# Loading x and context ahead of the constants, and placing the k and q products inside the next chunk's w_ada tiles, in a two-layer float32 kernel

## The reference

```python
sh1, sc1, g1, sh2, sc2, g2 = adaln(c, w_ada, b_ada)          # silu(c) @ w_ada + b_ada, split in 6
h = modulate(rms_norm(x, norm_mix_g), sh1, sc1)               # y * (1 + scale) + shift
csh1, csc1, ... = adaln(c_ctx, w_ada, b_ada)
hc = modulate(rms_norm(ctx, norm_mix_g), csh1, csc1)
q, k, v = split(h @ w_qkv, 3);  qc, kc, vc = split(hc @ w_qkv, 3)
```

## Time and profile before

| | us |
|---|---|
| median of 3 runs (2806.07 to 2807.3) | 2806.37 |
| the profiled execution | 2807.16 |
| its span, first to last instruction | 2805.4 |
| PE busy | 2711.4 (97%) |
| DVE busy | 1580.2 (56%) |
| ACT busy | 1174.5 (42%) |

### The profile page before, as it was taken

One profiled execution on the slowest core, in us unless ns is written; L12 is line 12 of the kernel. 1 busy time (PEld: TensorE's weight loads), 2 busy tenths in 40 slices (PEclk: granted clock), 3 DMA queues, 4 the chain that ended last, 5 costly groups with the idle time before them and its releaser, 6 DMA issues.

```text
span 2805.4 us, 47582 instructions
## 1 busy us (share of the span) xinstructions
PE 2711.4 (97%) x20374; PEld 2564.8 (91%) x20374; DVE 1580.2 (56%) x2407; ACT 1174.5 (42%) x1473; POOL 83.1 (3%) x85
## 2 busy tenths in 40 slices
PE   6999999999979999999999799999999999999999
PEld 3688888889979999999999698999988889999999
DVE  2466766665468765456554665655544555444554
ACT  2233333333345444344543344454535445434443
POOL 0010000000000000000000000000000000000000
PEclk9999999999999999999999799999999999999999
DMA  9955666663548875555555255445444345555554
GB/s 298 356 180 175 205 198 205 204 208 126 168 158 266 257 226 185 181 184 185 181 175 175 93 173 158 151 154 155 142 122 129 120 136 165 181 184 184 172 181 158
DMA packets 382138, 508.79 MB, mean 181 GB/s; under 512 B 40697, under 2 KB 252281, under 8 KB 381927
## 3 DMA queue, kind: packets, MB, share of 16 engines
q1 hardware_dynamic: 380215, 502.17, 55.8%
q0 software_dynamic: 1712, 3.58, 0.6%
HBM read 503.44 MB, written 2.22 MB: 180 GB/s over the span
## 4 chain that ended last, share of the span: by engine, by line
PE 90%; DVE 3%; ACT 3%; issue 2%; DMA 1%; SPq 1%; DVEq 0%; ACTq 0%
PE PG L852 23%; PE PG L853 23%; PE PG L854 23%; PE PG L843 3%; PE PG L845 3%; PE PG L844 3%; ACT wh L1095 1%; PE PS L945 1%; PE PS L861 1%; PE PS L929 1%; SPq L706 1%; PE PX L768 1%; PE PS L872 1%; DMA raw<-in_w_qkv 1%; PE PS L897 1%
## 5 line engine op out<-in xcount | busy, mean ns | idle before, releaser
L1410 DVE TENSOR_TENSOR wl<-raw,wh 128x1024 fp32r<-128x1024 f32 x748 | 917.5, 1227 | 984.4 <-ACT wh L1095 982.2
L1095 ACT ACTIVATE wh<-raw 128x1024 fp32r<-128x1024 f32 x748 | 790.4, 1057 | 1237.6 <-PE PG L854 1017.1
L852 PE MATMUL PG<-HHL,wh 128*128 128x256 f32 (+1 forms) x1696 | 499.7, 295 | 5.9 <-DVE HHL L1537 5.9
L853 PE MATMUL PG<-HHL,wh 128*128 128x256 f32 (+1 forms) x1696 | 488.4, 288 | 0.0
L854 PE MATMUL PG<-HHL,wl 128*128 128x256 f32 (+1 forms) x1696 | 488.3, 288 | 0.0
L852 PE MATMUL PG<-FHL,wh 128*128 128x256 f32 x1376 | 391.7, 285 | 9.0 <-DVE wl L1410 6.9
L853 PE MATMUL PG<-FHL,wh 128*128 128x256 f32 x1376 | 390.9, 284 | 0.0
L854 PE MATMUL PG<-FHL,wl 128*128 128x256 f32 x1376 | 390.8, 284 | 0.0
L852 PEld LDWEIGHTS PG<-HHL,wh 128*128 128x128 f32 (+1 forms) x1696 | 332.9, 196 | 12.2 <-issue 5.8
L853 PEld LDWEIGHTS PG<-HHL,wh 128*128 128x128 f32 (+1 forms) x1696 | 333.0, 196 | 2.5 <-issue 1.9
L854 PEld LDWEIGHTS PG<-HHL,wl 128*128 128x128 f32 (+1 forms) x1696 | 332.7, 196 | 0.1
(11 more groups left out here) (324 smaller groups left out, 5071.4 us busy)
## 6 DMA issues: line engine op xcount, KB each, us to landing
raw<-in_w_in SPq DMA_DIRECT2D x208, 512.0 KB, 3.4
raw<-in_w_up SPq DMA_DIRECT2D x344, 256.0 KB, 3.1
raw<-in_w_ada SPq DMA_DIRECT2D x128, 512.0 KB, 4.6
raw<-in_w_down SPq DMA_DIRECT2D x84, 512.0 KB, 3.6
raw<-in_w_qkv SPq DMA_DIRECT2D x80, 512.0 KB, 4.7
first<-in_w_ada SPq DMA_DIRECT2D x82, 256.0 KB, 7.1
raw<-in_w_o SPq DMA_DIRECT2D x32, 512.0 KB, 3.6
raw<-in_w_in SPq DMA_DIRECT2D x64, 256.0 KB, 3.0
```

Source lines behind the costliest of these rows:

```text
L852: pe.matmul(dst, hi[:, c0:c1], xh, start=step.first and j % per == 0, stop=False, skip_group_check=True)
L853: pe.matmul(dst, hi[:, c0:c1], xl, start=False, stop=False, skip_group_check=True)
L1095: ac.activation(wh[n % NSPL][:, 0:src.shape[1]], src, ACT.Copy).then_inc(S["hi"], 1)
L1410: dv.tensor_tensor(wl[n % NSPL][:, 0:x], src, wh[n % NSPL][:, 0:x], ALU.subtract).then_inc(S["lo"], 1)
```

## The change

x and context are issued first by SP. The condition vectors and the 20 remaining constants are issued by ACT, ahead of its first instruction; the ones matrix is no longer loaded but written by GpSimd. The wait for all the constants moves from the `energy` matmuls to L881. The steps of `early` and the order of the tiles move:

```diff
--- before.py
+++ after.py
@@ -161,9 +161,8 @@
         qkv, rest = mats[KC:n_qkv], mats[n_qkv:]
         plan = []
         for c in range(NCH):
-            plan += chunk_tiles(c)
-            if c:
-                plan += mats[2 * c - 2:2 * c]
+            tiles = chunk_tiles(c)
+            plan += tiles[:2] + (mats[2 * c - 2:2 * c] if c else []) + tiles[2:]
         plan += mats[KC - 2:KC]
         self.start = len(plan)
         late = [t for c in range(2 * D, 5 * D, ADA_W) for t in ada_tiles(c)]
@@ -196,8 +195,8 @@
             for n in range(8 * c, 8 * c + 8):
                 self.at["chunk", n, 0] = len(self.steps)
                 self.steps.append(Step("chunk", n))
-            if c:
-                self.early(c - 1)
+                if c and n % 8 == 3:
+                    self.early(c - 1)
         self.early(NCH - 1)
         for p, (name, g, k0, nk, tiles) in enumerate(self.prods):
             k = 0
@@ -268,8 +267,7 @@
                 P.put(at, 0, "mod", (z, ch), 0)
             for z in "xc":
                 P.put(at, 0, "mod", (z, ch), 1)
-        at = ("chunk", 8 * c + 10, 0) if c < NCH - 1 else ("early", NCH - 2, 0)
-        P.put(at, 0, "split", 2 * c + 1, 0)
+        P.put(("chunk", 8 * c + 8, 0) if c < NCH - 1 else at, 0, "split", 2 * c + 1, 0)
     at = ("early", NCH - 1, 0)
     P.put(at, 0, "split", KC, 0)
     for job, g in (("k_out", 0), ("k_out", 1), ("q_out", 0), ("q_out", 1)):
@@ -674,7 +672,7 @@
     def up_view(g, blk):
         return result("up", g)[:, blk // 2, T * (blk % 2):T * (blk % 2) + T]
 
-    consts = ((ident, "ident"), (ones, "ones"), (means, "means"), (sel, "sel"), (na_mask, "na_mask"), (caus_q, "caus_q"),
+    consts = ((ident, "ident"), (means, "means"), (sel, "sel"), (na_mask, "na_mask"), (caus_q, "caus_q"),
               (caus_k, "caus_k"), (rot, "rot"), (freq, "freq"), (bada, "b_ada"), (gmix, "g_mix"), (gffn, "g_ffn"),
               (gqk, "g_qk"), (g2, "g_in"), (mg, "g_ml"), (glat, "g_lat"), (gn, "g_nope"), (gr, "g_rope"),
               (cw2, "conv2"), (gb, "gate_b"), (rpbt, "rpb"))
@@ -682,13 +680,9 @@
 
     def sync(sp):
         w = Waits(sp)
-        sp.dma_start(CS[:, :, :], I["conds"]).then_inc(S["cond"], 16)
+        sp.dma_start(X[:, :, :], I["xT"].rearrange("(c p) t -> p c t", p=128)).then_inc(S["xload"], 16)
+        sp.dma_start(XC[:, :, :], I["ctxT"].rearrange("(c p) t -> p c t", p=128)).then_inc(S["cload"], 16)
         for i, (kind, name, k, nk, segs) in enumerate(plan):
-            if i == 0:
-                for dst, src in consts:
-                    sp.dma_start(dst[tuple(slice(None) for _ in dst.shape)], I[src]).then_inc(S["const"], 16)
-                sp.dma_start(X[:, :, :], I["xT"].rearrange("(c p) t -> p c t", p=128)).then_inc(S["xload"], 16)
-                sp.dma_start(XC[:, :, :], I["ctxT"].rearrange("(c p) t -> p c t", p=128)).then_inc(S["cload"], 16)
             j = P.slot_before[i]
             if j is not None:
                 n = P.index[j]
@@ -715,12 +709,13 @@
 
     def gpsimd(po):
         w = Waits(po)
+        po.memset(ones[:, :], 1.0).then_inc(S["pool"], 1)
         po.memset(CSP[:, :, :], 0.0).then_inc(S["pool"], 1)
         po.memset(padt[:, :, :], 0.0).then_inc(S["pool"], 1)
-        w.wait_ge(S["pool"], 2)
+        w.wait_ge(S["pool"], 3)
         w.wait_ge(*const_done)
         po.tensor_copy(padt[:, :, 48:79], rpbt[:, :, :]).then_inc(S["pool"], 1)
-        w.wait_ge(S["pool"], 3)
+        w.wait_ge(S["pool"], 4)
         po.dma_start(pad_dram[0:30720].rearrange("(a p n) -> p a n", a=2, n=128), padt[:, :, :]).then_inc(S["pad"], 16)
         w.wait_ge(S["pad"], 16)
         w.wait_ge(*product_done("early", 0))
@@ -865,7 +860,7 @@
             ps = bank(u)
             if (job, phase) == ("energy", 1):
                 z, j = key
-                w.wait_ge(*const_done)
+                w.wait_ge(S["pool"], 1)
                 w.wait_ge(S["energy_sq"], nth("energy", key, 0))
                 for ch in range(4):
                     o = T * (z == "c")
@@ -873,6 +868,7 @@
                                     start=z == "x" and j == 0 and ch == 0, stop=j == 3 and ch == 3, skip_group_check=True)
                 end.then_inc(S["energy"], 1)
             elif (job, phase) == ("rows", 1):
+                w.wait_ge(*const_done)
                 w.wait_ge(S["ada_row"], key + 1)
                 w.wait_ge(S["rx"], 1)
                 if key:
@@ -1362,9 +1358,12 @@
                 ac.activation(VHL[:, 0, 2 * key:2 * key + 2, :], GA[:, 2 * key:2 * key + 2, :],
                               ACT.Copy).then_inc(S["y_hi"], 1)
 
+        ac.dma_start(CS[:, :, :], I["conds"]).then_inc(S["cond"], 16)
+        for dst, src in consts:
+            ac.dma_start(dst[tuple(slice(None) for _ in dst.shape)], I[src]).then_inc(S["const"], 16)
         w.wait_ge(S["cond"], 16)
         ac.activation(CSs[:, :, :], CS[:, :, :], ACT.Silu).then_inc(S["silu_c"], 1)
-        w.wait_ge(S["pool"], 1)
+        w.wait_ge(S["pool"], 2)
         ac.activation(CSP[:, :, 0:2], CS[:, :, :].rearrange("p z k -> p k z"), ACT.Silu).then_inc(S["silu_c"], 1)
         for s, step in enumerate(steps):
             if step.kind == "mat" and step.opens:
@@ -1920,7 +1919,7 @@
 
 def constants():
 
-    c = {"ident": np.eye(128), "ones": np.ones((128, 128))}
+    c = {"ident": np.eye(128)}
     c["means"] = np.tile(1.0 / np.array([2048, 512, 256, 192, 128, 192, 192]), (128, 1))
     c["sel"] = np.stack([np.arange(128) % 32 == z for z in range(2)], 1)
     c["means"][64:, 5] = 0.0
```

## The result

| | before | after |
|---|---|---|
| median of 4 runs each, side by side | 2806.39 us (2806.07 to 2807.3) | 2850.76 us (2843.01 to 2857.13) |
| profiled execution, its span | 2807.16, 2805.4 | 2843.01, 2841.2 |
| L881, now L877, of chunk 0 | 45.23 | 39.62 |
| the same of chunk 7 | 144.32 | 192.85 |
| start of early(7) | 156.28 | 201.36 |

The change makes the kernel slower: ratio 1.0156, with a 95% interval of 1.0131 to 1.0182. The forecast was 2850. The front gained 5.6 us by L881 of chunk 0 (45.23 to 39.62); from there to L881 of chunk 7 the chunks lost 54.1.

The account below looks back on a forecast made before the run. First stage bound by transfers, the rest by PE. Front gains 7.4 us, loops take 21.5 us against 14.9, so early(7) comes 41.2 us later; 2.1 more for its clock gives +43.3, median 2850 us; range 2829 to 2866.

Parts of the forecast that it names:

- The front: Kernel start: x loaded first, constants issued by ACT; first square and L881(0) 7.4 us earlier, between 1.4 and 10.2.
- the clock's fall: PE in each of eight chunks: half clock after a 5.7 us wait, costing 2.1 us each, 3.4 at most.
- closed loop: First stage: early(c) stands between L881(c) and L881(c+1), so a chunk takes 19.4 us against 14.9, 21.5 with the clock.
- The rival of transfers that go on bounding the stage: First stage: tile stream starts 10.2 us earlier and stays full; 2793 us, chance 0.04.
- The row at 239 us: Kernel before: after 4.6 us idle the clock was 0.50, returning 4.2 us after PE went on; gave the 2.1 us.
- the row where the clock held: Kernel before, ahead of 156.28 us: after 2.46 us idle the clock stayed at 1.00; by it the term is nothing.
- The case without a fall: Rival for the first stage: front gains 7.4 us, loops take 19.4 at full clock; 2833 us, chance 0.12.
- As long as ACT is later than x: Kernel start: condition under which constants sharing the DMA engines with x, context and first tiles cost nothing.
- The loops: First stage, L881(0) to L881(7): seven loops of 21.5 us, 150.5, plus 0.6 for chunk 0.
- a tail of unchanged length: From early(7) to the end: program the same, so the +43.3 us shift carries to the end.
- The range: Whole kernel: 2829 to 2866 us, covering the forecast (own range 2838 to 2862) and the case without the clock's fall.
- "Nothing" for the order of the tiles: First stage: w_qkv tiles moved ahead of six w_ada tiles land some microseconds sooner, DVE not ready; no effect.

Follow-up runs that it names:

- e1: Kernel after with the chunk, tile and split order of the kernel before, leaving only the front of the change: 2798.23 us, ratio 0.9964.
- e2: Kernel before with only the new order of tiles, steps and splits, its front unchanged: 2857.16 us, ratio 1.0184.
- e7: Kernel after with each chunk's splits ahead of its rows and mod pieces on ACT and DVE: 2816.53 us, ratio 1.004.
- e6: Kernel after with early one chunk later, early(c-2) standing where early(c-1) stood: 2806.98 us, ratio 1.0005.
- e9: e6 with the tiles in the order of the kernel before: 2798.03 us, ratio 0.9978.
- e5: Kernel after with 10 unused filler matmuls on PE behind each L877 (14 ahead of early(7)): 2836.3 us, ratio 1.0107.
- e8: e1 with the 20 constants issued by GpSimd and not by ACT: 2799.29 us, ratio 0.9972.
- e10: Kernel after with the tiles in the order of the kernel before: 2855.88 us, ratio 1.0178.
- e4: Kernel after with early behind seven of the next chunk's eight tiles and not four: 2837.6 us, ratio 1.011.
- e3: Kernel after with 20 unused filler matmuls on PE behind each L877 (28 ahead of early(7)): 2864.92 us.

## Why the prediction was right

Times of the profiled executions, in us:

| step | forecast | measured |
|---|---|---|
| X from issue to landing | 8.55 | 9.8 |
| end of ACT's 21 issues | 10.5 | 11.9 |
| first square of x | 12.1 | 13.48 |
| L877(0) | 37.8 | 39.62 |
| L877 to early | 8.6 | 8.5 |
| early in the loop, with the clock's fall | 8.3 + 2.1 | 10.4 |
| half of the tiles, copy | 2.45 | 2.7 |
| a loop | 21.5 | 21.9 (seven of 21.0 to 22.9) |
| early(7) against before | +41.2 | +45.1 |
| DMA share of the stage | 0.75 | 0.76 |
| waits before early | 8, 5 to 6 | 8: 3.9, six of 5.5 to 5.6, 7.5 |
| from early(7) to the end | unchanged | 9.3 us shorter |
| median of the runs against before | +44 | +44.4 |

**The mechanism.** A closed loop took the place of transfers as the bound. The kernel after shows it in the eight waits for `wl`; e1 and e2 put the whole loss into the order. e7 shortens the path from L877 to early by 2.8 us and e6 and e9 open the loop; the time follows each. The rival of transfers that go on bounding the stage (2793) would have needed loops of 14.8 us.

**The clock.** Its term was 8 times 2.1, 16.8 us; e5 measures about 14.5 in all. In the loop of chunk 3, early loses the 2.1 of the forecast. The row at 239 us was the right one to lean on, the row where the clock held was not: its idle time was 2.46 us, less than half of that here. The case without a fall (2833) is what e5 builds, and it came to 2836. The Trainium skill (TensorE: Matmul & The Clock Gate, section on HAM oscillation) says that such a loop starts cold at every turn; in this loop the trace agrees, with 0.50 at the start of early and a gain of 14.5 us when the wait is filled. In the shorter waits of e7 (2.8 to 2.9 us) it doesn't at every turn: the clock fell behind two of six.

**The front: the term that was mis-sized.** The forecast took 0.47 us for each of ACT's issues, SP's mean. They took 0.53 us (11.2 us for 21). That put the first square at 13.48, and it took 0.5 us longer than before from there to L877(0): the front gained 5.6 us, not 7.4. "As long as ACT is later than x" held, since x had landed at 10.5 us. But x took 9.8 us and not 8.55. That fits the constants beside it, whose queue took 15.1% of the DMA engines' time in the first 11 us; no run loads x without them (9.9 us in e8, where GpSimd issues them). The Trainium skill (DMA: Bandwidth & Descriptors, section on issuing engines that are not separate DMA queues) says that all issuers' transfers interleave on the same 16 engines; these rows agree.

**The loops.** From L877(0) to L877(7) the forecast had 151.1 us; it is 153.2. The first loop took 22.9, since PE stood at 0.50 from 37 to 54 us there and all of its work up to the middle of early ran at the low clock; the others took 21.0 to 22.6, depending on when in early the clock came back. With the front's 1.8 us that makes the 3.9 us by which early(7) is later than forecast. In the medians it doesn't show: +44.4 against +44. The two agree better than the steps do: the profiled execution was 45.1 us late at early(7) and 35.8 at the end, where the prediction had a tail of unchanged length. The range was earned by the mechanism; the agreement to 0.4 us is in part luck.

**"Nothing" for the order of the tiles.** Near enough in the closed loop, where the DMA engines have time to spare (e10: at most a few us saved). As a statement on the edit it is wrong: with the loop open it costs 9 us (e6 against e9, 6.6 of them seen inside the stage), through the buffers that tiles hold when they land before they can be used; the prediction saw that DVE wouldn't be ready for them, and not what that costs.

**Still open.** What makes the runs spread isn't settled. Those of the kernel after lie 14 us apart, but so do those of e1 and e6, without the eight waits, and the kernel before has 1.2 us in four runs on one chip and 9 to 11 in 14 to 22 on the others; filling the waits (e5) narrowed them little, to 11 us, while the four runs each of e4, e7 and e10 lie 2 to 4 us apart. Which of the later waits decide whether the clock falls wasn't tried.

## What to carry to other kernels

A product that needs the result of a row of small pieces must stand at least as much of PE's work behind them as the pieces take; moved nearer, it turns two engines that work side by side into two that take turns. Count that path (here 8.6 us) against what stands between (here 2.9 us) before moving anything, and price the wait twice: once as idle time, and once more for the lower clock behind it (here a third of the loss). A load that is moved ahead of its use isn't free in a ring where transfers are the bound (e6): it holds a buffer for the whole time.

## What the hardware showed that was not expected

- One f32 matmul of 128x256 shows as two records 0.22 us apart: 20 instructions gave 40 records and 8.88 us (e3), 10 gave 20 and 4.56 us (e5).
- DMA issues of small constants took 0.53 us each on ACT and 0.54 us on GpSimd (e8), against 0.47 us on SP in the kernel before.
- All eight earlies of the kernel after began at a clock of 0.50 behind their wait, but how long it stayed low differed: 17.1 us around chunk 0, 6.8 us in six of the chunks 1 to 7, and 3.4 us in chunk 4, whose loop was the shortest (21.0 us).
- Whether the clock fell went with the length of the wait. Ahead of or just behind the start of early(1) to early(6), it fell at six of six waits of 5.5 to 5.6 us (kernel after), at six of six of 3.8 to 3.9 us (e4), at two of six of 2.8 to 2.9 us (e7) and at none of 1.1 to 1.2 us (e5).
- Runs of one kernel differ by up to 14 us, and the mean granted clock goes with it: the kernel after took 2843.0 us at 0.978 and 2857.1 us at 0.971.
